# w_mod slabs in the normed tokens' idle buffers, and context queries two head pairs at a time

## The reference, cut to what matters

```python
def _layer(x, cond, prm, ctx):
    mod = silu(cond) @ w_mod + b_mod                       # 6 x D_MODEL columns, for c and c_ctx
    sh1, sc1, g1, sh2, sc2, g2 = split(mod, 6)
    h = rmsnorm(x, g_mix) * (1 + sc1) + sh1
    qa, ka, va, qc, kc, vc, u, gb, gc, pv, gates = project(h, w_in, ...)
    # context tokens read only context tokens; latent tokens read the cached context keys and all
    # latent keys (att_a) or a window of +-128 (att_c, with a sink logit per head)
    att_a, att_c = attend(qa, ka, va), attend(qc, kc, vc, sink)
    br = stack([att_a, short_conv(u, gb, gc), att_c, pool_mix(pv)])
    x = x + g1 * (sum(gates * (br @ w_br)) @ w_o)
    h2 = rmsnorm(x, g_ffn) * (1 + sc2) + sh2
    a, b = split(h2 @ w_gu, 2)
    return x + g2 * ((silu(a) * b) @ w_down)
```

## Time and profile before

| | us |
|---|---|
| median of three runs (lowest, highest) | 1495.55 (1494.07, 1497.26) |
| the profiled execution, its time | 1497.93 |
| its span in the profile | 1496.2 |
| TensorE busy (PE), weight loads (PEld) | 1448.5, 1380.7 |
| VectorE, ScalarE, GpSimd busy | 876.0, 592.5, 183.7 |
| matmuls of the units with `h` (L737 + L738 + L739) | 570.3 + 558.3 + 558.5 |

### The profile page before, as it was taken

How to read it: one execution, slowest core, us unless ns; L and a number is a source line. 1 busy time by engine, 2 the same in 40 slices (tenths; PEclk the granted TensorE clock), 3 DMA queues, 4 the chain that set the end, 5 groups by cost and what they waited for, 6 DMA issues and landing times.

```text
span 1496.2 us, 26292 instructions
## 1 busy us (share of the span) xinstructions
PE 1448.5 (97%) x9053; PEld 1380.7 (92%) x9053; DVE 876.0 (59%) x1653; ACT 592.5 (40%) x1102; POOL 183.7 (12%) x173
## 2 busy tenths in 40 slices
PE   5999999999999999999978999999999999999998
PEld 4899999998888999999968999999999989999998
DVE  4776666643444877777757766666443575455333
ACT  3544545442333433332224444544432453333322
POOL 2220120111222000000002200201132300000000
PEclk7999999999999999999989999999999999999999
DMA  9732123257666555546663321233344734342341
GB/s 314 212 120 86 57 85 114 86 165 215 205 224 204 184 182 169 194 149 228 208 206 101 120 85 62 80 114 103 109 122 146 233 106 139 115 139 88 109 133 53
DMA packets 208909, 215.59 MB, mean 144 GB/s; under 512 B 7896, under 2 KB 202776, under 8 KB 208664
## 3 DMA queue, kind: packets, MB, share of 16 engines
q1 hardware_dynamic: 178616, 168.50, 36.0%
q10 hardware_dynamic: 29760, 44.57, 9.0%
q0 software_dynamic: 416, 1.05, 0.2%
HBM read 211.98 MB, written 2.11 MB: 143 GB/s over the span
## 4 chain that ended last, share of the span: by engine, by line
PE 81%; DVE 7%; issue 6%; ACT 2%; DMA 2%; ACTq 1%; DVEq 0%; POOL 0%; POOLq 0%
PE bank L737 24%; PE bank L739 23%; PE bank L738 23%; DVE unread L1395 3%; PE tr L902 2%; PE sc L880 2%; ACT w_hi L1048 2%; DMA mod_w<-in_w_mod 2%; PE tr L889 2%; DVE w_lo L1289 1%; PE sc L808 1%; PE tr L838 1%; ACTq L607 1%; DVE ff_f L1321 0%; DMA tok<-in_x_prompt 0%
## 5 line engine op out<-in xcount | busy, mean ns | idle before, releaser
L737 PE MATMUL bank<-h_hi,w_lo 128*128 128x384 f32 x1664 | 570.3, 343 | 11.3 <-DVE h_lo L1294 6.6
L739 PE MATMUL bank<-h_hi,w_hi 128*128 128x384 f32 x1664 | 558.5, 336 | 0.0
L738 PE MATMUL bank<-h_lo,w_hi 128*128 128x384 f32 x1664 | 558.3, 336 | 0.0
L1289 DVE TENSOR_TENSOR w_lo<-raw,w_hi 128x1024 fp32r<-128x1024 f32 (+3 forms) x352 | 385.8, 1100 | 293.3 <-ACT w_hi L1048 292.6
L1048 ACT CAST w_hi<-raw 128x1024 fp32r<-128x1024 f32 (+3 forms) x352 | 322.4, 922 | 126.4 <-PE bank L739 103.0
L737 PEld LDWEIGHTS bank<-h_hi,w_lo 128*128 128x128 f32 x1664 | 313.7, 188 | 25.1 <-issue 13.0
L738 PEld LDWEIGHTS bank<-h_lo,w_hi 128*128 128x128 f32 x1664 | 314.1, 189 | 0.0
L739 PEld LDWEIGHTS bank<-h_hi,w_hi 128*128 128x128 f32 x1664 | 313.7, 189 | 0.0
L737 PE MATMUL bank<-br_hi,w_lo 128*128 128x384 f32 (+1 forms) x384 | 132.2, 344 | 3.3 <-DVE br_lo L1295 3.3
L739 PE MATMUL bank<-br_hi,w_hi 128*128 128x384 f32 (+1 forms) x384 | 128.7, 335 | 0.0
L738 PE MATMUL bank<-br_lo,w_hi 128*128 128x384 f32 (+1 forms) x384 | 128.6, 335 | 0.0
(11 more groups left out here) (189 smaller groups left out, 1317.5 us busy)
## 6 DMA issues: line engine op xcount, KB each, us to landing
raw<-in_w_in SPq DMA_DIRECT2D x120, 512.0 KB, 4.5
raw<-in_w_gate_up SPq DMA_DIRECT2D x88, 512.0 KB, 4.4
mod_w<-in_w_mod ACTq DMA_DIRECT2D x36, 512.0 KB, 5.1
raw<-in_w_down SPq DMA_DIRECT2D x48, 384.0 KB, 3.7
mod_t<-in_w_mod_t ACTq DMA_DIRECT2D x34, 512.0 KB, 3.3
raw<-in_w_branch SPq DMA_DIRECT2D x64, 256.0 KB, 3.7
raw<-in_w_out SPq DMA_DIRECT2D x16, 512.0 KB, 4.6
start_w<-in_w_mod SPq DMA_DIRECT2D x12, 512.0 KB, 8.7
```

Of the source, the lines that this page charges most:

```text
L737: pe.matmul(out, w[1], r[0], start=start, stop=False)
L738: pe.matmul(out, w[0], r[1], start=False, stop=False)
L739: return pe.matmul(out, w[0], r[0], start=False, stop=stop)
L1289: dve.tensor_tensor(to, src, hi.bitcast(F32), ALU.subtract).then_inc(lo_ready.sem, 1)
```

## The change

Attention has 20 blocks per layer instead of 24. The 16 latent blocks stay; the 8 context blocks become 4, each for two head pairs c, with all of their scores, exponentials, transposes and outputs in one step. The order is now by m, first its 8 latent blocks, then its 2 merged context blocks. Steps are 43 instead of 51, over the same units. VectorE's maximum, reciprocal and rest, ScalarE's copies and the sink's exponentials work on both head pairs at once; the exponentials and scalings stay one per head.

The three w_mod slabs of the boundary all are loaded in the down stage's slot 4. Slabs 0 and 1 go into the memory of `h_hi` and `h_lo`, which nothing reads after the last gate-up unit, so they wait for that unit instead of the last dot.

```diff
+NA = 20
+
+
+def attention_step(i):
+
+    m, r = i // 10, i % 10
+    if r < 8:
+        return m, [r // 2], r % 2
+    return m, [2 * (r - 8), 2 * (r - 8) + 1], 2
...
-    for k in range(51):
+    for k in range(2 * NA + 3):
         now, j = [], k // 2
         if k % 2 == 0:
             now += [("attn", j - 2)] if j >= 2 else []
-            now += [("scores", j)] if j < 24 else []
+            now += [("scores", j)] if j < NA else []
         else:
-            now += [("scale", j)] if j < 24 else []
+            now += [("scale", j)] if j < NA else []
...
-    hooks[base["down"] + 2] += [("load_tail_next", 2)]
-    hooks[base["down"] + 2 * (DOTS - 20)] += [("load_tail_next", 0), ("load_tail_next", 1)]
+    hooks[base["down"] + 4] += [("load_tail_next", x) for x in range(3)]
...
         h_hi = place("h_hi", [P, DC, T], F32R)
+        tail_h0 = place("tail_h0", [P, SLAB], at=place.end - DC * T * 4)
         h_lo = place("h_lo", [P, DC, T], F32R)
+        tail_h1 = place("tail_h1", [P, SLAB], at=place.end - DC * T * 4)
...
-        dot_sums = place("dot_sums", [P, 2, 2])
+        dot_sums = mod_sums[:, 0, :, :]
...
-        tail_slab = [mod_w[:, 0, :], mod_w[:, 1, :], tail_w[:, :]]
+        tail_slab = [tail_h0[:, :], tail_h1[:, :], tail_w[:, :]]
...
+        def attended(to, i):
+
+            m, cs, t = attention_step(i)
+            return to[:, 8 + 4 * m + cs[0]:9 + 4 * m + cs[-1], P * t:P * t + P]
+
+        def attn_bank(i):
+
+            n = len(attention_step(i)[1])
+            return tr[:, 0, 512 - P * n:512].rearrange("p (c q) -> p c q", c=n)
...
                 elif what == "scores":
-                    m, c, t = i // 12, i % 12 // 3, i % 3
-                    pe.wait_ge(*qk_split(l, 2 + 4 * m + c))
+                    m, cs, t = attention_step(i)
+                    pe.wait_ge(*qk_split(l, 2 + 4 * m + cs[-1]))
                     pe.wait_ge(*past_split(l, m))
                     if i:
                         pe.wait_ge(*exps(l, i - 1))
                     ks = slice(0, PAST + T_LAT) if t < 2 else slice(PAST + T_LAT, PAST + T)
-
-                    for r, (q_, k_) in enumerate(((q_lo, k_hi[:, m, :]), (q_hi, k_lo[m]), (q_hi, k_hi[:, m, :]))):
-                        for g in range(2):
-                            a = slice(64 * g, 64 * g + 64)
-                            ins = pe.matmul(sc[:, g, 0:ks.stop - ks.start], q_[a, 4 * m + c, P * t:P * t + P], k_[a, ks],
-                                            start=r == 0, stop=r == 2)
+                    nk = ks.stop - ks.start
+
+                    for n, c in enumerate(cs):
+                        for r, (q_, k_) in enumerate(((q_lo, k_hi[:, m, :]), (q_hi, k_lo[m]), (q_hi, k_hi[:, m, :]))):
+                            for g in range(2):
+                                a = slice(64 * g, 64 * g + 64)
+                                ins = pe.matmul(sc[:, g, nk * n:nk * n + nk], q_[a, 4 * m + c, P * t:P * t + P], k_[a, ks],
+                                                start=r == 0, stop=r == 2)
                     ins.then_inc(scores.sem, 1)
...
-                        for b in range(3 if i % 3 < 2 else 1):
+                        for b in range(3 if attention_step(i)[2] < 2 else 2):
...
                     tiles = (0, 1, 2) if t < 2 else (3,)
-                    for b, v in enumerate(tiles):
-                        for g in range(2):
-                            ins = pe.matmul(tr[64 * g:64 * g + 64, 0, 384:512], vals[:, m, v, 64 * g:64 * g + 64],
-                                            prob_t[:, i % 2, g, b, :], start=b == 0, stop=v == tiles[-1])
+                    for n in range(len(cs)):
+                        to = slice(512 - P * (len(cs) - n), 512 - P * (len(cs) - n) + P)
+                        for b, v in enumerate(tiles):
+                            for g in range(2):
+                                ins = pe.matmul(tr[64 * g:64 * g + 64, 0, to], vals[:, m, v, 64 * g:64 * g + 64],
+                                                prob_t[:, i % 2, g, b + n, :], start=b == 0, stop=v == tiles[-1])
                     ins.then_inc(attn_out.sem, 1)
...
-                    act.wait_ge(*(ff_split(l, FC - 1) if i == 2 else dot_both(0, DOTS - 1)))
+                    act.wait_ge(*(ff_split(l, FC - 1) if i == 2 else unit_done(l, N_D - 1)))
                     load_mod(act, tail_slab[i], (l + 1) % DEPTH, slice(256 * (DOTS // 2 + i), 256 * (DOTS // 2 + i + 1)),
...
-                    nk = PAST + T_LAT if i % 3 < 2 else T_CTX
-                    c = 2 + 4 * (i // 12) + i % 12 // 3
-                    for g in range(2):
-                        r = 2 * (i % 3) + g
-                        ins = act.activation(prob[:, i % 2, g, 0:nk], sc[:, g, 0:nk], ACT.Exp, scale=q_rs[:, c, r:r + 1],
-                                             bias=s_nm[i % 2][:, g:g + 1], accum_out=s_sum[i % 2][:, g:g + 1])
+                    m, cs, t = attention_step(i)
+                    nk = PAST + T_LAT if t < 2 else T_CTX
+                    for n, c in enumerate(cs):
+                        for g in range(2):
+                            k, r = len(cs) * g + n, 2 * t + g
+                            ins = act.activation(prob[:, i % 2, g, nk * n:nk * n + nk], sc[:, g, nk * n:nk * n + nk], ACT.Exp,
+                                                 scale=q_rs[:, 2 + 4 * m + c, r:r + 1], bias=s_nm[i % 2][:, k:k + 1],
+                                                 accum_out=s_sum[i % 2][:, k:k + 1])
                     ins.then_inc(exps.sem, 1)
-                    if i >= 12:
-                        act.activation(s_se, s_sd, ACT.Exp).then_inc(sink_exp.sem, 1)
+                    if m:
+                        act.activation(s_se[:, 0:2 * len(cs)], s_sd[:, 0:2 * len(cs)], ACT.Exp).then_inc(sink_exp.sem, 1)
...
-                    s = chain.made(dve.reduce_max(s_max, sc[:, :, 0:nk], AXX))
+                    s = chain.made(dve.reduce_max(s_max[:, 0:2 * n].rearrange("p (g c) -> p g c", g=2),
+                                                  sc[:, :, 0:n * nk].rearrange("p g (c k) -> p g c k", c=n), AXX))
...
-                    s = chain.made(dve.reciprocal(s_r, total))
+                    s = chain.made(dve.reciprocal(s_r[:, 0:2 * n], total))
                     dve.wait_ge(*s)
-                    for g in range(2):
-                        v = prob[:, i % 2, g, 0:nk]
-                        ins = dve.tensor_scalar(v, v, s_r[:, g:g + 1], None, ALU.mult)
+                    for k in range(2 * n):
+                        v = prob[:, i % 2, k // n, nk * (k % n):nk * (k % n) + nk]
+                        ins = dve.tensor_scalar(v, v, s_r[:, k:k + 1], None, ALU.mult)
                     ins.then_inc(probs_ready.sem, 1)
...
-                    lo_part(br_lo[:, 8 + 4 * m + c, part], tr[:, 0, 384:512], br_hi[:, 8 + 4 * m + c, part])\
-                        .then_inc(attn_ready.sem, 1)
+                    lo_part(attended(br_lo, i), attn_bank(i), attended(br_hi, i)).then_inc(attn_ready.sem, 1)
```

More of the change, by code:

```diff
@@ L394, in program @@
         nsink = place("nsink", [P, NQ])
-        st = place("st", [P, 64])
+        st = place("st", [P, 80])
         exponent = place("exponent", [P, 1])
         mod_sums = place("mod_sums", [P, 6, 2, 2])
-        dot_sums = place("dot_sums", [P, 2, 2])
+        dot_sums = mod_sums[:, 0, :, :]
         q_rs = place("q_rs", [P, 10, 2 * TT])
@@ L402, in program @@
         q_ms = [st[:, 8 + 8 * i:14 + 8 * i] for i in range(2)]
-        s_max, s_nm = st[:, 40:42], [st[:, 42 + 2 * i:44 + 2 * i] for i in range(2)]
-        s_sum = [st[:, 46 + 2 * i:48 + 2 * i] for i in range(2)]
-        s_sd, s_se, s_r = st[:, 50:52], st[:, 52:54], st[:, 54:56]
+        s_max, s_nm = st[:, 40:44], [st[:, 44 + 4 * i:48 + 4 * i] for i in range(2)]
+        s_sum = [st[:, 52 + 4 * i:56 + 4 * i] for i in range(2)]
+        s_sd, s_se, s_r = st[:, 60:64], st[:, 64:68], st[:, 68:72]
         ident = const[:, K_ID:K_ID + P]
@@ L436, in program @@
         past_turned = signal("past_turned", 2)
-        scores = signal("scores", 24)
-        probs_turned = signal("probs_turned", 24)
-        attn_out = signal("attn_out", 24)
+        scores = signal("scores", NA)
+        probs_turned = signal("probs_turned", NA)
+        attn_out = signal("attn_out", NA)
         mod_sum = signal("mod_sum", 0)
@@ L457, in program @@
         qk_hi = signal("qk_hi", 10)
[L458 to L461, removed]
+        exps = signal("exps", NA)
+        sink_exp = signal("sink_exp", NA // 2)
+        probs_t_ready = signal("probs_t_ready", NA)
+        attn_hi = signal("attn_hi", NA)
         mod_row_ready = signal("mod_row_ready", 0)
@@ L487, in program @@
         v_ready = signal("v_ready", 2)
-        max_ready = signal("max_ready", 24)
-        probs_ready = signal("probs_ready", 24)
-        attn_ready = signal("attn_ready", 24)
+        max_ready = signal("max_ready", NA)
+        probs_ready = signal("probs_ready", NA)
```

(32 more changed lines are left out.)

22 lines of the change are left out of this document (11 added, 11 removed).

## The result

The changed kernel took 1485.62 us (median of 4 runs, 1482.37 to 1486.11), the kernel before, run beside it, 1494.81 (4 runs, 1493.51 to 1497.26). The ratio is 0.9927, 95% interval 0.9916 to 0.9939: 10.9 us less, between 9.1 and 12.6; the two medians lie 9.2 apart. The forecast was 10.9 less and 1484.6. The total came out, and two of its terms did not: the down stage cost more than twice what was set down for it, and attention gave more.

The account below looks back on a forecast made before the run. Attention was taken as bound by its matmuls, the down stage by a ScalarE-VectorE loop, the boundary by slab waits. Terms −9.4 + 2.8 − 3.9 − 0.4 = −10.9 took 1495.55 to 1484.6 us, range 1480.5 to 1489.7.

Parts of the forecast that it names:

- The boundary: Between layers 1 and 2: with slabs present, first projection at 774.41 instead of 783.79, 9.4 us less.
- the low bound of 7.2: Layer boundary: if the clock stays at the low level throughout, only the wait goes, 7.2 us.
- another wait takes its place: Rival at the layer boundary: slabs are there but another wait leaves half of the 9.4; 1489.4 us, chance 0.05.
- The down stage: Layer 1's down stage: six load issues in a row on ScalarE delay casts and w_lo, net 2.8 us more.
- grows by more than 5 us: Sign that the prediction is wrong: layer 1's down stage grows by more than 5 us.
- issues held longer: Rival in the down stage: two of six issues take 2.90 us each, 4.5 more; 1489.2 us, chance 0.12.
- with nothing to catch it up: Down stage: the loop through ScalarE and VectorE sets the pace, so a delay in it counts in full.
- The clock rival: Rival: clock drops in new pauses before units 8 and 9, stays low through the boundary; 1486.9 us, chance 0.05.
- The row of eight: Eight same-shape loads in a row elsewhere in the trace, used to price the down stage's six issues at 3.76 us.
- Attention: Both layers' attention: 18 combined steps between projection matmuls instead of 22, 3.9 us less, plus 0.4 for a wait.
- The wait: Attention: one TensorE wait of 0.4 us per layer, half of 0.8 counted as gain, 0.4 us.
- The forecast case: Whole kernel: all terms as set down, 10.9 us less, 1484.6 us, chance 0.56.

Follow-up runs that it names:

- e4: Changed kernel with the six w_mod slab loads issued by SyncE behind three w_down slabs, none by ScalarE: 1476.91 us, ratio 0.9876.
- e8: Changed kernel with context blocks one at a time again (24 blocks per layer) but in the new order: 1489.42 us, one run.
- e7: Changed kernel with the six loads reading w_mod_t in 4 KB rows instead of w_mod in 1 KB rows, same bytes: 1482.05 us, one run.
- e6: Changed kernel with tail_w's two loads back in slot 2, so four issues stand in a row in slot 4: 1481.27 us, one run.
- e2: Changed kernel with the w_mod loads as in the kernel before, so attention's part alone: 1488.01 us, ratio 0.9957 against the kernel before.

## Why the prediction was right, and which steps were not

**The boundary** (−9.4): −9.45. Square to statistics 0.90, square to `nx` 4.26 and `nx` to projection 2.28 against 0.90, 4.25 and 2.29. A template from elsewhere in the same trace gave the stage within 0.1 us. The clock stood at 1.00, so the low bound of 7.2 does not apply, and with the whole 9.4 won the rival "another wait takes its place" falls as well.

**The down stage** (+2.8): +6.74. This is the step that failed, and by the prediction's own mark ("grows by more than 5 us"). The place, the engine, and the chain from issue to cast to `w_lo` to TensorE were right; the price of the six issues was not. They took 684.12 to 691.80, 7.7 us, instead of 3.76. The mechanism is that of the rival "issues held longer", at a price of its own: 5.41 for the last two where it had two at 2.90. With the measured distance of the two casts, 691.99 − 683.87 = 8.12, in place of its 0.26 + 3.76 + 0.1, the prediction's own working gives 8.12 − 0.73 − 0.6 = 6.8, and the stage grew by 6.74. So the delay did count in full, "with nothing to catch it up", and only the size of the row was wrong. The other kernels bear this out: against e4, where ScalarE issues none of the six, the stage is 7.55 longer here, 6.65 in e8 and 2.78 in e7, and ScalarE's idle time ahead of the cast of unit 8 is 7.40, 6.64 and 2.83.

The clock rival was half right: the clock fell in the new pause, but it was back at 1.00 at the boundary. Where it was low, 12 matmuls stood 0.32 instead of 0.17 apart, 1.76 in all, and this added nothing to the stage: the `w_lo` of unit 9, late by the same hold, was finished at 699.04, and unit 9's first matmul started at 699.11.

```profile
698.08 0.96 DVE L1316 TENSOR_TENSOR w_lo<-raw,w_hi 128x768 fp32r<-128x768 f32 x1 [1.20 <-ACT w_hi L1074]
```
```profile
699.11 0.43 PE L759 MATMUL bank<-f_hi,w_lo 128*128 128x384 f32 x1
```

At full clock TensorE would have waited there, as it does in e6, where the clock stayed at 1.00 (1.80 at 694.26). The row of eight misled because its first six issues went unhindered; here the queue had a `mod_t` load 0.7 us before, and the w_down slabs were being moved beside it. Which of these made the hold start two issues earlier was not taken apart.

**Attention** (−4.3 with the wait): −5.69 over the two layers in the profiles, and −5.95 (2.96 and 2.99) without layer 1's wait for `mod_w`, which is no part of it. The prices of the merged steps were 1.82 and 1.51 against 1.81 and 1.51 forecast, so the count of steps stands. The wait went in full: none is listed after, and in e8, without the merging, 0.3 stays; I had counted half. Of layer 2's 2.99, 1.96 is the count of steps and 0.4 the wait; the other 0.6 is not placed. It comes with the merging (e8 gives 0.11 of 2.99 to the order).

**The rest.** The gate and up stage is 1.0 shorter, for which nothing was set down; 0.6 of it comes with the merged blocks (e2 183.24 and e8 183.84): a wait of TensorE for `w_lo` late in the stage (0.36 before, one of the six of the earlier trace rows; 0.15 in e8) is gone with them. Why it goes was not looked into. The start of the program, 1.8 earlier in the profile, is scatter.

**The total** was right by luck, because two errors nearly cancel: 3.9 too little cost in the down stage, and some 2.4 too little gain in and right behind attention. They alone make −10.9 + 3.9 − 2.4 = −9.4, near the 9.2 between the medians. The profiled pair differs by 11.8, because in it the start of the program is 1.8 earlier and the stages outside the table give another 0.6. The forecast case, with its mean of 0.63 per issue, did not happen; the case of the longer issues did, and attention's larger gain brought it back to the forecast's time. Of the 9.5 that the change wins at the boundary it pays 6.7 in the stage before: issued by SyncE, the same loads lengthen nothing (e4, 95.90).

## What to carry to other kernels

Loads that an engine issues are work in its order: look for what stands behind them, and for a loop that closes over that engine, before you put several in one place. Price a row of issues by how many pieces the queue already holds, and spread them, give them longer rows, or let an engine issue them behind which no matmul waits. For a stage whose wait is to be taken out, a place in the same trace where the same chain runs without that wait gives the new length almost exactly; for a moved piece of work there was no such place, and the nearest row, of another stretch, gave half of the number.

## What the runs showed of the hardware

- DMA issues of 512 KB in rows of 1 KB took 0.5 us each on ScalarE for the first four in a row (2.10), and 5.41 for the fifth and sixth in a row; in rows of 4 KB none was held (e7). With two earlier loads still under way, already the first four took 2.97 instead of 2.10 (e6), and SyncE's third pair 2.26 instead of 0.94 (e4).
- After 5.36 us without work TensorE's granted clock was 0.50 in the next 4 us, and matmuls of 384 columns stood 0.32 apart. Shorter pauses did both: 1.10 and 2.14 between starts in e6 left the matmuls 0.17 apart, 1.13 and 2.13 in e7 brought ten at 0.32 (granted clock 0.58 from 694 to 698). What decides between these two was not settled.
